# A DeltaNet and attention block on one core: the output projection and the last FFN product in two passes of 256 tokens

## The reference, cut to what matters

```python
y = merged @ w_out
x = x + mod[5] * rmsnorm(y, mix_post)
h = rmsnorm(x, ffn2_pre) * (1 + mod[7]) + mod[6]
a, b = split(h @ w_gu, 2)
y = (silu(a) * b) @ w_down
x = x + 0.5 * mod[8] * rmsnorm(y, ffn2_post)
```

## Time and profile before

| | |
|---|---|
| median of three runs | 2066.08 us |
| profiled execution, its own time | 2054.03 us |
| span of its profile | 2052.4 us |
| PE busy | 1964.0 us (96%) |
| DVE busy | 1127.2 us (55%) |
| ACT busy | 810.0 us (39%) |
| POOL busy | 283.9 us (14%) |
| DMA traffic, mean | 85 GB/s |
| DMA traffic, first fortieth of the span | 316 GB/s |
| loads of weight blocks | 221 of 512 KB |

### The profile page before, as it was taken

The page is one execution under the profiler, slowest core; times in us unless marked ns, Lnnn a source line. Parts: engine busy times, 40 slices in busy tenths (PEclk is TensorE's granted clock), DMA queues, the critical chain, the costliest instruction groups (busy, mean ns, idle before and its releaser), DMA issues.

```text
span 2052.4 us, 30685 instructions
## 1 busy us (share of the span) xinstructions
PE 1964.0 (96%) x11073; PEld 1680.9 (82%) x11073; DVE 1127.2 (55%) x2047; ACT 810.0 (39%) x1241; POOL 283.9 (14%) x234
## 2 busy tenths in 40 slices
PE   7899999999996999999999999998999979999996
PEld 3788888888884779988888888887888858888885
DVE  5777655555446565566676667666433353233335
ACT  4312222211225556565466546654422352222223
POOL 0000000000000120042543355233000000000000
PEclk9999999999998999999999999999999999999998
DMA  8233333333221330011011101100222312222222
GB/s 316 83 116 120 123 123 123 123 123 123 92 72 59 118 101 25 1 57 46 21 56 38 38 36 50 42 31 22 92 92 102 133 52 93 102 92 102 92 97 77
DMA packets 49035, 174.72 MB, mean 85 GB/s; under 512 B 6724, under 2 KB 6852, under 8 KB 48720
## 3 DMA queue, kind: packets, MB, share of 16 engines
q1 hardware_dynamic: 37632, 129.95, 17.8%
q0 software_dynamic: 11344, 43.97, 6.3%
HBM read 167.03 MB, written 4.24 MB: 83 GB/s over the span
## 4 chain that ended last, share of the span: by engine, by line
PE 89%; DVE 4%; ACT 3%; issue 3%; DMA 1%; POOL 0%; SPq 0%; DVEq 0%; ACTq 0%; POOLq 0%
PE ps L1393 82%; PE ps L1397 4%; PE ps L1725 1%; PE ps L1646 1%; DMA w_first<-WMOD 1%; PE ps L1779 1%; DVE X L917 1%; DVE n_y L909 1%; ACT n_t L508 1%; DVE w_lo L835 0%; PE ps L1681 0%; ACT d_qu L748 0%; DVE m_part L1018 0%; ACT h_hi L512 0%; ACT w_hi L444 0%
## 5 line engine op out<-in xcount | busy, mean ns | idle before, releaser
L1393 PE MATMUL ps<-h_hi,w_hi 128*128 128x512 f32 (+1 forms) x1712 | 548.3, 369 | 20.1 <-DVE h_lo L892 11.3
L444 ACT ACTIVATE w_hi<-raw 128x1024 fp32r<-128x1024 f32 x221 | 234.0, 1059 | 800.7 <-PE ps L1393 795.7
L1393 PE MATMUL ps<-h_lo,w_hi 128*128 128x512 f32 (+1 forms) x1712 | 536.2, 360 | 0.0
L1393 PE MATMUL ps<-h_hi,w_lo 128*128 128x512 f32 (+1 forms) x1712 | 528.7, 359 | 0.0
L835 DVE TENSOR_TENSOR w_lo<-raw,w_hi 128x1024 fp32r<-128x1024 f32 x221 | 279.3, 1264 | 411.7 <-ACT w_hi L444 411.6
L1393 PEld LDWEIGHTS ps<-h_hi,w_hi 128*128 128x128 f32 x1712 | 319.1, 190 | 75.9 <-issue 20.5
L1393 PEld LDWEIGHTS ps<-h_lo,w_hi 128*128 128x128 f32 x1712 | 323.5, 189 | 49.2 <-issue 3.4
L1393 PEld LDWEIGHTS ps<-h_hi,w_lo 128*128 128x128 f32 x1712 | 323.5, 189 | 48.8
L1393 PE MATMUL ps<-g_hi,w_hi 128*128 128x512 f32 (+1 forms) x528 | 158.4, 354 | 0.0
L1393 PE MATMUL ps<-g_lo,w_hi 128*128 128x512 f32 (+1 forms) x528 | 157.8, 353 | 0.0
L1393 PE MATMUL ps<-g_hi,w_lo 128*128 128x512 f32 (+1 forms) x528 | 157.8, 353 | 0.0
(11 more groups left out here) (265 smaller groups left out, 2678.8 us busy)
## 6 DMA issues: line engine op xcount, KB each, us to landing
raw<-W SPq DMA_DIRECT2D x221, 512.0 KB, 3.4
w_mod<-WMOD POOLq DMA_DIRECT2D x56, 512.0 KB, 3.7
w_mod<-WMOD SPq DMA_DIRECT2D x12, 512.0 KB, 15.4
g_row<-g_rows POOLq DMA_DIRECT2D x8, 768.0 KB, 4.5
X<-XT SPq DMA_DIRECT2D x4, 768.0 KB, 7.1
a_sw<-i_n POOLq DMA_DIRECT2D x40, 64.0 KB, 1.9
w_first<-WMOD SPq DMA_DIRECT2D x4, 512.0 KB, 12.6
x_spill<-X POOLq DMA_DIRECT2D x1, 2048.0 KB, 7.8
```

The lines of the kernel that those rows point to most:

```text
L444: a.activation(w_hi[:, b.pair], raw[:, b.raw], ACT.Copy).then_inc(s("w_hi"), 1)
L1393: return pe.matmul(out, lhsT, rhs, start=start, stop=stop)
```

## The change

The output projection and the last down part (c == 2 of the second FFN) run in two passes: all 8 blocks over the first 256 tokens, then the 8 blocks again over the second 256. So their weight blocks stand twice in the list, are loaded twice and split twice: 16 blocks more (the weight array is built with w_out and the last down weights twice). The norms are cut into halves of 256 tokens as well, and the instructions of the first half's norms are written between the blocks of the second pass. A second pair of split buffers (w_hx, w_lx) is used for the blocks in SPARE, and POOL makes the remainder w_lo, in DVE's place, for the blocks in POOL_LOW: blocks 10 to 15 of the output projection, the first 4 of the FFN, and the second pass of the last down part. In that last part only 6 of 8 tiles are split (`depth`). The first four FFN blocks, each in its own bank, are done as a group: blocks 0 and 1 over the first half of the tokens, blocks 2 and 3 over the first half, then all four over the second half (`first_up`). The sums over partitions of 256 columns (`y_sum`, `x_sum`) stand inside PE's stream. The table of ACT's functions for the last norm is loaded before the last down part. Stores go out by halves, 8 in place of 4. Loops of these stretches are written out.

```diff
-B_FFN2 = B_OUT + KT
-NBLK = B_FFN2 + N_FFN
+B_FFN2 = B_OUT + 2 * KT
+B_LAST = B_FFN2 + N_FFN - KT
+NBLK = B_LAST + 2 * KT
+HALF = SEQ // 2
+SQ_AT, FOLD_AT, SS_AT, X_AT = {"o": 8, "f": 24}, {"o": 9, "f": 24}, {"o": 1, "f": 3}, {"o": 8, "f": 24}
+RS_AT = {("o", 0): 3, ("x", 0): 4, ("o", 1): 5, ("x", 1): 6, ("f", 0): 7, ("f", 1): 8}
+SPARE = {b + j for b, js in ((B_OUT, (10, 11, 14, 15)), (B_FFN2, (2, 3)), (B_LAST, (2, 3, 6, 7, 10, 11, 14, 15))) for j in js}
+POOL_LOW = [list(range(B_OUT + KT + 2, B_FFN2 + 4)), list(range(B_LAST + KT, NBLK))]
...
+        def weights(b):
+
+            if isinstance(b.n, int) and b.n in SPARE:
+                return w_hx[:, b.pair], w_lx[:, b.pair]
+            return w_hi[:, b.pair], w_lo[:, b.pair]
...
-            for k in range(0, KT, 2):
-                sp.wait_ge(s("x_new"), 2 * KT + k + 2)
-                sp.dma_start(OUT.rearrange("(k p) t -> p k t", p=P)[:, k:k + 2], X2[:, k:k + 2]).then_inc(s("stored"), 16)
-            sp.wait_ge(s("stored"), 16 * (KT // 2))
+            for h in range(2):
+                for k in range(0, KT, 2):
+                    sp.wait_ge(s("x_new"), X_AT["f"] + KT * h + k + 2)
+                    sp.dma_start(OUT.rearrange("(k p) t -> p k t", p=P)[:, k:k + 2, xhalf(h)], X2[:, k:k + 2, xhalf(h)])\
+                      .then_inc(s("stored"), 16)
+            sp.wait_ge(s("stored"), 16 * KT)
...
+            for blocks in POOL_LOW:
+                for n in blocks:
+                    b = Blk(n, 0, 0)
+                    kt = depth(b)
+                    hi, lo = weights(b)
+                    g.wait_ge(s("w_split"), n)
+                    g.wait_ge(s("w_hi"), n + 1)
+                    g.tensor_tensor(lo[:, 0:kt], raw[:, b.raw, 0:kt], hi[:, 0:kt].bitcast(F32), ALU.subtract).then_inc(s("w_split"), 1)
...
+            def last_down():
+                blks = [Blk(B_LAST, 0, i) for i in range(2 * KT)]
+                for i, blk in enumerate(blks):
+                    if i + 2 < 2 * KT:
+                        if i >= 2:
+                            a.wait_ge(s("gemm_done"), blks[i - 2].n + 1)
+                        split(blks[i + 2])
+                    a.wait_ge(psum_read[blk.pair], blk.turn + 2)
+                    y_square("f", i, Y2[:, i % KT, xhalf(i // KT)])
+                    if i == KT:
+                        y_rstd("f", 0)
+                y_rstd("f", 1)
...
-            loop(a, KT // 4, out_proj)
-            all_read(a, B_OUT + KT)
-            rstd(3, CTX)
-            pre_norm(4, 2, CTX)
+            for i in range(KT):
+                step(out[i])
+                out_read(i)
+            for i in range(KT, 2 * KT):
+                if i >= KT + 2:
+                    a.wait_ge(s("gemm_done"), out[i - 2].n + 1)
+                split(out[i + 2])
+                out_read(i)
+                if i == KT:
+                    for b in out[KT - 2:KT]:
+                        a.wait_ge(psum_read[b.pair], b.turn + 2)
+                    y_rstd("o", 0)
+                for k in {9: (0,), 10: (1, 2), 11: (3, 4, 5, 6), 12: (7,)}.get(i, ()):
+                    x_square(0, k)
+                if i == 13:
+                    x_rstd(0)
+                if i == 14:
+                    h_tile(0, 0)
+                    h_tile(0, 1)
+            for b in out[2 * KT - 2:2 * KT]:
+                a.wait_ge(psum_read[b.pair], b.turn + 2)
+            for k in range(2, KT):
+                h_tile(0, k)
+                if k < 4:
+                    split(out[2 * KT + k])
+                if k == 4:
+                    y_rstd("o", 1)
+            for k in range(KT):
+                x_square(1, k)
+            x_rstd(1)
+            for k in range(KT):
+                h_tile(1, k)
...
+            def last_down():
+                blks = [Blk(B_LAST, 0, i) for i in range(2 * KT)]
+                v.wait_ge(s("ss_ready"), SS_AT["o"] + 2)
+                v.memset(y_acc[:], 0.0).then_inc(s("ysq_used"), 1)
+                for i, blk in enumerate(blks):
+                    v.wait_ge(s("gemm_done"), blk.n + 1)
+                    yk = Y2[:, i % KT, xhalf(i // KT)]
+                    v.tensor_tensor(yk, yk, bank(blk, 1)[:, 0:HALF], ALU.add).then_inc(psum_read[blk.pair], 1)
+                    if i + 2 < KT:
+                        split(blks[i + 2])
+                    if i % KT:
+                        y_fold("f", i - 1)
+                    if i > KT:
+                        x_add("f", 2, 0, i - KT - 1)
+                x_add("f", 2, 0, KT - 1)
+                for k in range(KT):
+                    x_add("f", 2, 1, k)
...
-            def out_proj(it):
-                for j in range(4):
-                    step(Blk(B_OUT, it, j))
-                    if not (isinstance(it, int) and it == KT // 4 - 1 and j == 3):
-                        v.wait_ge(s("ysq"), it * 4 + (KT + j + 1))
-                        v.wait_ge(s("ysq_used"), it * 4 + (8 + j + 2))
-                        v.tensor_tensor(y_acc[:, CTX:T], y_acc[:, CTX:T], (m_a, m_b)[j % 2][:], ALU.add).then_inc(s("ysq_used"), 1)
             v.memset(y_acc[:], 0.0).then_inc(s("ysq_used"), 1)
-            loop(v, KT // 4, out_proj, True)
+            for i in range(KT):
+                step(Blk(B_OUT, 0, i))
+                if i < KT - 1:
+                    y_fold("o", i)
             v.wait_ge(s("x_back"), 16)
-            post_norm(3, 1, CTX)
-            pre_norm(4, 2, CTX)
-            ffn(1, B_FFN2, segs_x, True)
-            post_norm(5, 2, CTX)
+            y_fold("o", 8)
+            for i in range(9, 13):
+                x_add("o", 1, 0, 2 * (i - 9))
+                x_add("o", 1, 0, 2 * (i - 9) + 1)
+                y_fold("o", i)
+            y_fold("o", 13)
+            for k in range(KT):
+                h_low(0, k)
+                if k == 1:
+                    y_fold("o", 14)
+            for k in range(KT):
+                x_add("o", 1, 1, k)
+            for k in range(KT):
+                h_low(1, k)
+            ffn(1, B_FFN2, segs_x)
...
+            def first_up():
+                blks = [Blk(B_FFN2, 0, j) for j in range(4)]
+                for k in range(KT):
+                    if k == 2:
+                        y_sum("o", 1)
+                    for j in range(2):
+                        first_slice(blks[j], j, 0, k)
+                for k in range(KT):
+                    for j in range(2, 4):
+                        first_slice(blks[j], j, 0, k)
+                    if k >= 2:
+                        x_sum(1, k - 2)
+                x_sum(1, KT - 2)
+                x_sum(1, KT - 1)
+                for k in range(KT + 2):
+                    for j in range(4):
+                        if 0 <= k - j // 2 * 2 < KT:
+                            first_slice(blks[j], j, 1, k - j // 2 * 2)
...
-            def out_proj(it):
-                for j in range(4):
-                    gemm(Blk(B_OUT, it, j), m_hi, m_lo, segs_x, off=CTX, ready=(s("m_ready"), 0) if j == 0 else None)
-            loop(pe, KT // 4, out_proj)
-            sum_partitions(3, CTX)
-            sum_squares(4, CTX)
+            for n in range(2 * KT):
+                h = n // KT
+                gemm(Blk(B_OUT, 0, n), m_hi, m_lo, [(CTX + HALF * h, CTX + HALF * h + HALF, 1)], off=CTX,
+                     ready=(s("m_ready"), 0) if n == 0 else None)
+                if n == KT:
+                    y_sum("o", 0)
+                for k in {11: (0, 1, 2), 12: (3, 4, 5, 6), 13: (7,)}.get(n, ()):
+                    x_sum(0, k)
             ffn(1, B_FFN2, segs_x)
-            sum_partitions(5, CTX)
...
+                            if not first:
+                                step(blk)
+                            elif j < 2:
+                                a.wait_ge(s("gemm_done"), blk.n + 1)
+                                split(blk.ahead(4))
...
+            def x_square(h, k):
+                n = KT * h + k
+                a.wait_ge(s("x_new"), X_AT["o"] + n + 1)
+                if n >= 2:
+                    a.wait_ge(s("sq_used"), 2 * KT + n - 1)
+                a.activation(z_sq[:, k % 2], X2[:, k, xhalf(h)], ACT.Square).then_inc(s("sq_ready"), 1)
...
+            def first_slice(b, j, h, k):
+
+                if h == 0 and k == 0:
+                    pe.wait_ge(s("w_split"), b.n + 1)
+                    if j < 2:
+                        pe.wait_ge(psum_read[b.pair], b.turn + 1)
+                if j % 2 == 0:
+                    pe.wait_ge(s("h_ready"), 2 * KT + KT * h + k + 1)
+                wh, wl = weights(b)
+                for i, (w, x) in enumerate(((wh, h_hi), (wh, h_lo), (wl, h_hi))):
+                    last = mm(first_bank(b, j)[:, xhalf(h)], w[:, k, :], x[:, k, half(h)], k == 0 and i == 0, k == KT - 1 and i == 2)
...
+            def last_down():
+                for n in range(2 * KT):
+                    h = n // KT
```

(48 more changed lines are left out.)

148 lines of the change are left out of this document (128 added, 20 removed).

## The result

The changed kernel takes 2064.94 us, the median of 20 runs (2062.23 to 2074.86); the kernel before takes 2056.58 us in 20 runs (2053.78 to 2067.61). The ratio is 1.0038, 95% interval 1.0022 to 1.0053: the change costs 0.38%, some 8 us. In both kernels the times fall into two groups some 10 us apart (before: twelve runs around 2055.5 and eight around 2066; after: twelve around 2063.7 and eight around 2073.4); the numbers can't be read without this, because the profiled run of before is from the lower group and that of after from the upper one.

A forecast was written before the change was run, and what follows sets the result against it. PE's matmuls were taken as the bound, so only waits in two stretches could change: +5.2 (output projection through first four FFN blocks), +1.6 (clock), +1.2 (last part), +8.0 on 2066.1 gives 2074 us, range 2064 to 2081.

The forecast's parts named there:

- Its time is 12 us under the median shown; the difference carries over: Whole kernel: adds +8.0 us, found on the profiled execution (2054.0 to 2062.0), to the median 2066.1, giving 2074.
- PE's own work: Both stretches: 256-column matmuls 0.120 us each, sums 0.43; output projection through first four FFN blocks 73.9 becomes 77.7 us.
- that rival: Both stretches: 256-column matmuls take 109 ns, 864 of them saving 9 us; faster, 2058 us, chance 13%.
- the one with 0.175: Both stretches: weight loads set the pace at 0.175 us a matmul, 47 us more; 2120 us, chance 5%.
- Waits of A: Output projection, norms and first four FFN blocks: PE waits 17.8 us with restarts; stretch 90.3 becomes 95.5, +5.2.
- Item 3: Output projection's second pass: POOL and DVE hold each other up, so block 11's remainder comes 2.1 us late.
- Item 6: First half of h: ACT's work and DVE's remainder waiting for POOL twice cost PE 2.9 us over tiles 4 to 7.
- PE idle in A under 14 us: Sign of a wrong forecast: PE idling under 14 us from the output projection through the first four FFN blocks.
- Clock: Half-speed PE behind gaps of 2.1, 3.2 and 3.4 us, output projection through first four FFN blocks: +1.6, bounds 0 and 5.
- POOL and DVE: Each waits for the other to end: 2.1, 0.6 and 1.4 us up to FFN block 4, 2.9 in the last part.
- The 27% rival: Both stretches: POOL's subtraction hardly holds DVE up and the clock stays full; -0.4 us, 2065.7, chance 27%.
- B: Start of the last down part to the kernel's end: 50.4 us before, +1.2; last product 6.9 later, tail shorter.

The follow-up runs named there:

- gaps_filled: Changed kernel with 64 matmuls more, results unread, filling three gaps of PE from the output projection to the FFN's first blocks; ratio to before 1.0043, lower group 2062.7 us.
- last_two_pass: Kernel before with only the last down part in two passes, blocks loaded and split twice, POOL making second remainders; ratio to before 1.0012, lower group 2055.8 us.
- all_mended: Changed kernel, both stages begun with two blocks, output-projection-stage remainders on DVE, second FFN block's weights earlier, last part's weights kept; ratio to before 0.9988, lower group 2055.5 us.
- remainders_on_dve: Changed kernel with all 18 of POOL's remainders given back to DVE, POOL idle in both stages; ratio to before 1.0005, lower group 2057.0 us.
- two_blocks_first: Changed kernel, PE doing seven tiles of the output projection's first two blocks, then both eighths; second buffers for blocks 2, 3, 6, 7; ratio to before 1.0020.

## Why the prediction was right and wrong

**The absolute time: wrong.** Forecast 2074.0 and measured 2064.9, inside the range but 9 us off, where the change was forecast at +8.0 and is 0.38%, or 7.8 us. Against the 2056.6 that the kernel before takes in 20 runs, 2074 would have been +17.4, twice the 8.4 between the two medians. The step that failed is "Its time is 12 us under the median shown; the difference carries over". The three runs shown (2064.79 to 2067.61) all lay in the upper group; the profiled 2054.03 was in the lower one, with 12 of the 20 runs the commoner here. The 12 us were no cost that every execution pays on top of the profiled one, but 1.5 us of ordinary spread (to 2055.5) and 10.5 us between the groups, the size of what the first FFN's other pace takes in the traces. Right would have been to take two numbers so far apart for two kinds of execution, to add +8.0 to each (2062 and 2074, where the groups of after lie at 2063.7 and 2073.4) and to keep both in the range.

**PE's own work: right.** 256-column matmuls start 0.120 apart (1619.59, 1619.71), sums 0.43. The Trainium skill, "TensorE: Matmul & The Clock Gate", section Back-to-back issue gap, gives N / 2.4 + 2.5 ns for an isolated matmul, from which 109 ns is an estimate; in every run here it was 120 at the full clock, so that rival is dead. So is the one with 0.175.

**Waits of A.** Forecast and measured: m_lo 2.1 and 2.11; squares of x 0.5 and 0.17; block 1 of the FFN 3.2 and 3.51; second half of h 3.2 and 3.01; block 4 1.9 and 1.83. Item 3 put a wait of 2.1 at block 11, and there was none: that block's remainder ended at 1652.7, about a microsecond before PE came to it, since POOL kept its own pace and it was DVE that was pushed back. Item 6 forecast 2.9 over four tiles; the trace has 0.91 and 0.24 and a few of some 0.1. So 17.8 was too much by about 3: what is left of A's 97.4 without PE's 77.7 and the clock's 5.0 is 14.7. The prediction's own sign of being wrong, PE idle in A under 14 us, came: it is idle 12.2 (97.57 less 47.43 and 37.95).

**Clock: right in kind, too small.** I took +1.6 with bounds 0 and 5. The three stretches last 3.37, 3.31 and 3.52 us for work of 1.80, 1.51 and 1.92 at full clock: 5.0 us, the upper bound. The two misses, 3 us too much in the waits and 3.4 too little here, cancelled by luck: A was forecast +6.8 and measured +7.1. The fills show that these 5 us aren't simply to be had back.

**POOL and DVE: right and shown in B; in A right in kind, near in size by luck.** I had 4 us of it in A and 2.9 in B; giving the remainders back to DVE brought 3.1 and 2.9. But the largest part of the 4 us, item 3's 2.1 at block 11, never came, and nearly all of the 3.1 arises at the FFN's second block, 1.1 of it from POOL's 2.35 us against DVE's 1.23. The 27% rival (POOL hardly holds DVE up) is dead. The Trainium skill, "SBUF — State Buffer", section Who interferes with whom, says that a VectorE instruction with two SBUF inputs contends with a GpSimd instruction that reads SBUF, and that the shared port pair is an exclusive lock. These runs agree, with 2.62 us for a scale-and-add of 0.47.

**B: right.** Forecast +1.2, measured +0.9; last product 39.5 us after the start of the part and measured 39.7 to 39.9; tail 9.1 until DVE ends and then the store, measured 11.5 in all.

**What I didn't weigh.** That the cut by itself costs 6.8 us in A: I had its parts (2.6, 2.1, clock) but in separate items, and so didn't see that over half of the price is paid where the pass starts. The sum didn't suffer.

## What to carry to other kernels

Work that is handed to POOL to relieve DVE can cost more than it saves, when DVE has two-operand work from SBUF at the same time: price it as if both ran on one engine, and at POOL's duration. Price the narrower matmuls of a second pass first, then the norms that it hides. In the last down part it paid, by 2.2 us with the weights kept (B 48.3) and by 2.0 with them loaded and taken apart again, as long as DVE did that (48.5; before 50.5); in the output projection no version here got below the 90.3 of before. And where few runs and a profile disagree by more than the kernel's spread, look for a stage that takes two values before adding the difference to anything.

## What the runs showed of the hardware

The first FFN runs at one of two paces, with the granted clock at 1.00 in both. In the ten profiled runs of this case PE started 3057 to 3059 matmuls between 80 and 600 us in seven and exactly 3004 in three (after, last_two_pass, all_mended), and these three are the ones whose time lies in their kernel's upper group. By these counts (3058 over 3004) a pair of 512 and 256 columns takes 0.356 us at the slower pace, against the 0.350 of the earlier trace rows, an estimate. The second FFN doesn't have it: from block 4 to the last down part it takes 304.6 to 304.8 us in nine of the ten traces, the three among them (in gaps_filled, with a half-speed stretch there, 306.4). What sets it wasn't found.

A VectorE scale-and-add or addition of 128x256 with both inputs in SBUF, 0.41 to 0.48 us alone, took up to 2.6 us beside a GpSimd subtraction of 128x1024, and the subtraction 2.35 to 2.84. With nothing on GpSimd all 32 scale-and-adds lay between 477 and 487 ns.

Half-speed stretches of PE came behind waits of 4.56 us (before), 2.11, 3.51 and 3.01 us, not behind one of 1.80 (remainders_on_dve) nor of 1.50 (two_blocks_first), but also 2.15 us behind one of 1.86 and behind one of 1.83 (gaps_filled) and right behind two of 1.03 and 0.91 close together (all_mended).
